# A two-layer decoder trunk: weights split in their own place, eight raw weight places among the experts, and the last expert's share by a product instead of a gather

## The chip, the cores and the metric

One core of a Trainium2 chip runs the whole kernel as one program. The metric is the time of one execution in microseconds of device time (lower is better). Five engines work side by side, each through its own instruction stream and held together by semaphores that the kernel sets by hand: PE (matrix products, with weight loads shown apart as PEld), DVE (vector), ACT (scalar), POOL (GpSimd) and SP, which here only issues DMA transfers.

## The reference

Two groups of tokens, 512 of a prompt and 32 of samples, run together as T = 544 columns of width D = 1024. Layer 0 mixes tokens with a gated linear recurrence (RG-LRU), layer 1 with a gated delta rule (GDN). Each layer then attends to 256 memory tokens and ends in a channel mixer: layer 0 a dense SwiGLU, layer 1 the best two of eight expert SwiGLUs.

```python
def _trunk(x, mem_k, mem_v, lru_h, lru_conv, gdn_s, gdn_conv, p):
    for i in range(DEPTH):                       # DEPTH = 2
        if i % 2 == 0: mix, h, c = _rglru_mixer(x, ...)
        else:          mix, s, c = _gdn_mixer(x, ...)
        x = _layer_norm(DN_ALPHA * x + mix, ...)
        xa = _mem_attention(x, mem_k[i], mem_v[i], p['xa_wq'][i], p['xa_wo'][i])
        x = _layer_norm(DN_ALPHA * x + xa, ...)
        if i % 2 == 0: ff = _swiglu(x, w_gu, w_down, D_FF)          # 3072 hidden
        else:          ff = _moe_ffn(x, router, w_gu, w_down)       # 8 experts of 1536, top 2
        x = _layer_norm(DN_ALPHA * x + ff, ...)
```

`_moe_ffn` takes the softmax of a token's two best router logits as its two weights and adds the two experts' outputs with them.

## The kernel before

Weights lie in DRAM as slots of 128 x 1024 fp32 (512 KB), each one output tile of 128 columns (or its counterpart of a down projection). All 488 slots pass through one ring `raw` of four places, filled by SP in the order in which PE will use them. Stages in that order: key/value tiles of the memory (KV0), four LRU blocks, the LRU output (LOUT), queries and output of the first attention (Q, O), the dense SwiGLU in two halves of 36 slots (FFN), 32 GDN slots (four for each head), the GDN output (GOUT), Q and O of the second attention, and 8 x 36 slots of the experts. Key/value tiles of layer 1 lie between stages and fill PE's time in layer norms.

**Dense slots** are used in two parts. POOL makes a high part `wh` (fp32r) in four instructions (L527) and a low part `wl`, the raw weights less the high part, in four more (L531). PE then runs 48 matmuls of 272 columns (`lin_steps`, L625; in the FFN's down projection L865): high weights times high activations, low weights times high activations, high weights times low activations. `wh` and `wl` have two places each, so POOL waits in `split` until PE is through with the slot two before (`w_used`). SP refills a raw place as soon as POOL has split it (`w_split`). Key/value slots are used raw and never split. After a layer norm the first two slots of Q and FFN run interleaved on PE, because the normalised tiles arrive one by one (`linear`, `experts`); the first two slots of GOUT run together in the same way (`opening`), begun before the last head's output is there.

**Experts.** Tokens are sorted by expert into `rows_x` in DRAM. Experts stand in the order of their size with capacities 208 to 128 rows. The four largest (`wide_expert`) split their weights: ACT makes the high part, DVE the low part, into four places of their own. The four smallest (`expert`) use the raw weights in plain fp32 (L1235 up, L1252 down). SP refills a raw place when DVE has made its low part or, in the small experts, when PE has used it. A small expert's up projection gives two slots for each of 12 hidden tiles: ACT takes the silu (L1820), DVE multiplies (L2445, signalling `m_h`), and PE waits for that two tiles later. In its down projection the output tiles are evicted by ACT, turned by PE (`turn`, L1218) and copied by DVE (`turned`, L2438) into `M_y`. POOL stores `M_y` to `rows_y` in DRAM (L591).

**The end.** After the last expert's store has landed, POOL issues ten indirect gathers (L604), two for each of five token blocks (four of 128, one of 32), of the rows of each token's two experts. DVE adds them with their weights to the residual in two passes of 1024 columns (`statistics`, L2554), takes mean and variance (L2556, L2557) and normalises (L2562); PE turns the block back (L1327); ACT applies gain and bias in eight instructions (`columns`, L1874) and issues the store of y (L1877). On ACT the order is: factor of block t+1, then columns of block t.

Of the kernel before, what the change touches and what calls it, by code (L numbers as in the profile page):

```python
# [37 lines left out]
RAW, SPLIT, PIECES = 4, 2, 4  # L38
# [3 lines left out]
ZEROS = -(-ROWS // P)  # L42
PICKED, GATHERED = 6, 2
# [78 lines left out]
def trunk(nc, I, O):  # L122
# [5 lines left out]
    with ExitStack() as ctx:  # L128
# [14 lines left out]
        wh = sb("wh", [P, SPLIT, KT, P], R)  # L143
        wl = sb("wl", [P, SPLIT, KT, P], R)
# [286 lines left out]
        def _(sp):  # L431
            def load(t, offset, shift, lo=0, hi=RAW):


                for j in range(lo, hi):
# [7 lines left out]
            def turns(slot, n, before, own, dram):  # L443
                t0 = slot // RAW
                load(t0, before, dram - slot)
                if n > RAW:
                    with sp.Fori(t0 + 1, t0 + n // RAW) as t:
                        load(t, own, dram - slot)
# [9 lines left out]
            load(0, None, W_KV0)  # L458
            sp.wait_ge(w_in[0], 16)
            sp.dma_start(x[:, :, :], I["xT"]).then_inc(ld_x, 16)  # L460
            turns(S_KV0[1], RAW, None, None, W_KV0 + 4)
            turns(S_LRU[0], 2 * RAW, None, 8, W_LRU)
            turns(S_KV0[2], RAW, 8, None, W_KV0 + 8)
            turns(S_LRU[2], RAW, None, None, W_LRU + 8)
            turns(S_LRU[3], RAW, 12, None, W_LRU + 12)
            turns(S_KV0[3], RAW, 12, None, W_KV0 + 12)
            turns(S_LOUT, 8, None, 16, W_LOUT)
            turns(S_KV1[0], 4, 16, None, W_KV1)
            for l in range(NL):
                d = (20, 32)[l]  # L470
                turns(S_Q[l], 8, None, d, W_Q0 if l == 0 else W_Q1)
                turns(S_O[l], RAW, d, d, (W_Q0 if l == 0 else W_Q1) + 8)
                cache(l)
                turns(S_O[l] + RAW, RAW, d, d, (W_Q0 if l == 0 else W_Q1) + 8 + RAW)
                if l == 0:
                    turns(S_KV1[1], 4, 20, None, W_KV1 + 4)
                    turns(S_FFN, HALVES * 36, None, 24, W_FFN)
                    turns(S_KV1[2], 4, 24, None, W_KV1 + 8)
                    turns(S_GDN, 4 * GH + 8, None, 28, W_GDN)
                    turns(S_KV1[3], 4, 28, None, W_KV1 + 12)  # L480
# [20 lines left out]
            with sp.Else():  # L501
                for n in range(RAW, NE * 36):
                    if n - RAW < WIDE * 36:
                        sp.wait_ge(m_wl, WL + n + 1 - RAW)
                    else:
                        sp.wait_ge(w_used, S_MOE + n + 1 - RAW)
                    expert_slot(n)
# [5 lines left out]
        def _(pool):  # L513
# [4 lines left out]
            def split(t, first, offset):  # L518
# [15 lines left out]
            def turns(slot, n, first, offset):  # L534
                t0 = slot // RAW
                split(t0, first, offset)
# [6 lines left out]
            turns(S_Q[0], 16, 4, 20)  # L543
            turns(S_FFN, HALVES * 36, 4, 24)
            turns(S_GDN, 4 * GH + 8, 4, 28)
            turns(S_Q[1], S_MOE - S_Q[1], 4, 32)
# [5 lines left out]
            with pool.Else():  # L552
# [47 lines left out]
                pool.wait_ge(m_out, OUT_BY[NE - 1])  # L600
                for tt in range(NT):
                    n = P if tt < NC else NS
                    for m in range(2):
                        nc.gpsimd.indirect_dma_start(  # L604
                            out=Y_in[tt][m][0:n, :], out_offset=None, in_=rows_y,
                            in_offset=bass.IndirectOffsetOnAxis(ap=R_slot[0:n, m, tt:tt + 1], axis=0)).then_inc(c_in_y[tt], 16)
# [4 lines left out]
        def _(pe):  # L611
# [50 lines left out]
            def linear(slot, direct, ah, al, freed, base, fresh=None, opened=False):  # L662
# [9 lines left out]
                for s in range(2 if opened or fresh is not None else 0, 8):  # L672
                    if s >= 2:
                        pe.wait_ge(freed, base + s - 1)
                    lin_tile(slot + s, direct, s % 2, s % 2, ah, al)
# [142 lines left out]
            def experts(n, slot, direct, e0, first_ln):  # L818

                def one(e):  # L820
                    e36, e12, e8 = e * 36 + slot, (e + e0) * FT, (e + e0) * KT

                    def up(g):
# [12 lines left out]
                        for j in range(2 if opening else 0, 4):  # L836
# [3 lines left out]
                            lin_tile(e36 + g * 4 + j, direct, j % 2, j, xh, xl)  # L840
# [11 lines left out]
                    def down(g):  # L852
                        for q in range(4 * FT):
# [9 lines left out]
                            for m, (w, a) in enumerate(w_parts):  # L863
                                for h in range(2):
                                    last = mm(ps[:, 2 * d + h, 0:HT], w[:, s % 2, k, :], a[:, f, h * HT:(h + 1) * HT],  # L865
# [4 lines left out]
                    if isinstance(e, int) and e + e0 == 0:  # L870
                        down(0)
                        down(1)
                    else:
                        with pe.Fori(0, 2) as g:
                            down(g)
# [3 lines left out]
            def project(h, per=6, fresh=None):  # L879

                for j in range(4):
# [4 lines left out]
                    yield from lin_steps(S_GDN + 4 * h + j, 28, j % 2, 0, xh, xl, per=per, fresh=None if j else fresh)  # L886
# [11 lines left out]
            def lru_gel(b):  # L898

                for j in range(2):  # L900
                    pe.wait_ge(lru_ext, 2 * b + j + 1)
                    lin_tile(S_LRU[b] + 2 + j, 8 + 4 * (b // 2), j, j, xh, xl)
# [319 lines left out]

            def expert(r):
# [3 lines left out]
                for q in range(24):  # L1227
# [5 lines left out]
                    pe.wait_ge(w_in[slot % RAW], 16 * (slot // RAW + 1))  # L1233
# [1458 lines left out]
```

## Time and profile before

| | us |
|---|---|
| median of 3 runs (2505.19 to 2506.25) | 2506.08 |
| the profiled execution | 2509.16 |
| its span between first and last instruction | 2507.3 |
| PE busy | 2291.6 (91% of the span) |
| POOL busy | 1063.6 (42%) |

The profiled execution took 1.86 us more than its span, and 3.08 us more than the median of the runs. Times of the trace count from the span's start. By them the dense SwiGLU runs from about 470 to 923 us, the GDN stage to about 1530 us, GOUT to 1578 us, the experts' products from 1834 to 2459 us, and what follows them to 2507 us. A matmul's busy time is modelled and matmuls overlap, so PE at 100% means only that there was no gap.

### The profile page before, as it was taken

To read this page: it belongs to the slowest core of one execution; us is meant where nothing else is said; L and a number is where in the kernel's file an instruction comes from. 1 tells how busy PE (TensorE), PEld (TensorE's weight loads), DVE (VectorE), ACT (ScalarE), POOL (GpSimd) and SP (SyncE) were. 2 spreads that over 40 slices of the span, in tenths; PEclk is the share of its full clock that TensorE was granted. 3 is DMA by queue.
4 is the path that set the end of the run, shared out by engine and by line. 5 is a ranking of instruction groups with operands and counts; after the bars stand their busy time and mean duration, and the time that the engine had idled before them with its cause. 6 is when DMAs were issued, how large, how long until landed. Compare 5 with 4: busy or idle time off the path is not lost.

```text
span 2507.3 us, 43919 instructions
## 1 busy us (share of the span) xinstructions
PE 2291.6 (91%) x17238; PEld 2165.0 (86%) x17238; DVE 1134.6 (45%) x1739; ACT 720.5 (29%) x1218; POOL 1063.6 (42%) x1483
## 2 busy tenths in 40 slices
PE   8998889899999998999999778888799999999993
PEld 8988867899999996888888667867699999999993
DVE  3684412411011147777777644412557777410004
ACT  2352321311001114333333311321355666411103
POOL 4657434588888875433333105534221232100001
PEclk9999899899999998999999988999699999999996
DMA  7214442222222222211121102541176777778884
GB/s 296 100 60 162 154 165 85 93 84 84 89 88 84 89 90 69 69 55 62 62 63 63 45 27 88 194 165 68 52 256 208 260 249 264 238 247 280 285 285 161
DMA packets 98515, 347.22 MB, mean 138 GB/s; under 512 B 13488, under 2 KB 18864, under 8 KB 93472
## 3 DMA queue, kind: packets, MB, share of 16 engines
q1 hardware_dynamic: 73136, 279.08, 31.9%
q10 hardware_dynamic: 19472, 45.28, 5.2%
q0 software_dynamic: 5728, 20.38, 2.2%
q8 instruction: 122, 2.00, 0.3%
q14 instruction: 57, 0.47, 0.1%
HBM read 318.25 MB, written 26.47 MB: 137 GB/s over the span
## 4 chain that ended last, share of the span: by engine, by line
PE 64%; issue 15%; DVE 9%; POOL 6%; ACT 3%; DMA 3%; ACTq 0%; DVEq 0%; POOLq 0%; SPq 0%
PE ps L625 26%; PE ps L1262 8%; PE ps L1235 6%; PE ps L865 4%; PE ps L1264 4%; POOL wl L531 3%; PE ps L1252 3%; POOL wh L527 2%; DMA raw<-weights 2%; PE ps L726 1%; DVE x L1953 1%; PE ps L1076 1%; PE ps L1072 1%; PE ps L1055 1%; PE ps L730 1%
## 5 line engine op out<-in xcount | busy, mean ns | idle before, releaser
L527 POOL TENSOR_TENSOR wh<-raw,tab 128x256 fp32r<-128x256 f32 x672 | 438.8, 684 | 807.4 <-PE ps L625 543.5
L531 POOL TENSOR_TENSOR wl<-raw,wh 128x256 fp32r<-128x256 f32 x672 | 522.1, 808 | 0.0
L625 PE MATMUL ps<-xh,wh 128*128 128x272 f32 x2048 | 306.5, 300 | 47.1 <-POOL wl L531 15.5
L625 PEld LDWEIGHTS ps<-xh,wh 128*128 128x128 f32 x2048 | 276.8, 195 | 61.9 <-issue 24.5
L625 PE MATMUL ps<-xh,wl 128*128 128x272 f32 x2048 | 298.7, 296 | 0.0
L625 PE MATMUL ps<-xl,wh 128*128 128x272 f32 x2048 | 281.0, 289 | 0.0
L625 PEld LDWEIGHTS ps<-xh,wl 128*128 128x128 f32 x2048 | 277.1, 195 | 1.8 <-issue 0.5
L625 PEld LDWEIGHTS ps<-xl,wh 128*128 128x128 f32 x2048 | 266.2, 189 | 0.0
L1262 PE MATMUL ps<-moe_x,moe_wh 128*128 128x416 f32 (+3 forms) x768 | 214.5, 356 | 4.8 <-DVE moe_wl L2458 3.5
L2458 DVE TENSOR_TENSOR moe_wl<-raw,moe_wh 128x1024 fp32r<-128x1024 f32 x144 | 178.1, 1237 | 52.1 <-ACT moe_wh L1832 49.1
L1264 PE MATMUL ps<-moe_x,moe_wl 128*128 128x208 f32 (+3 forms) x768 | 188.9, 246 | 0.0
L1832 ACT ACTIVATE moe_wh<-raw 128x1024 fp32r<-128x1024 f32 x144 | 152.8, 1061 | 40.6 <-DMA raw<-weights 28.3
L1262 PEld LDWEIGHTS ps<-moe_x,moe_wh 128*128 128x128 f32 x768 | 144.1, 188 | 6.2 <-issue 3.4
L1264 PEld LDWEIGHTS ps<-moe_x,moe_wl 128*128 128x128 f32 x768 | 146.6, 191 | 0.0
L577 POOL CAST moe_hs<-work 128x208 fp32r<-128x208 f32 (+3 forms) x44 | 49.2, 1118 | 214.9 <-DVE work L2484 214.9
L591 POOL DMA_DIRECT2D rows_y<-moe_h x8 | 4.4, 549 | 319.7 <-DVE moe_h L2438 319.7
L2037 DVE TENSOR_TENSOR work<-work,ps 128x544 f32<-128x544 f32 x24 | 17.3, 722 | 228.6 <-PE ps L625 228.6
L1262 PE MATMUL ps<-moe_hs,moe_wh 128*128 128x416 f32 (+3 forms) x384 | 110.5, 360 | 0.0
L1235 PE MATMUL ps<-x,raw 128*128 128x144 f32 (+1 forms) x768 | 93.4, 284 | 3.6 <-DMA raw<-weights 3.6
L1235 PEld LDWEIGHTS ps<-x,raw 128*128 128x128 f32 x768 | 92.3, 194 | 4.3 <-issue 3.1
L1264 PE MATMUL ps<-moe_hs,moe_wl 128*128 128x208 f32 (+3 forms) x384 | 94.7, 247 | 0.0
L1252 PE MATMUL ps<-work,raw 128*128 128x128 f32 (+2 forms) x768 | 93.7, 279 | 1.0 <-DVE work L2445 0.8
(407 smaller groups left out, 3901.4 us busy)
## 6 DMA issues: line engine op xcount, KB each, us to landing
raw<-weights SPq DMA_DIRECT2D x488, 512.0 KB, 4.2
moe_h<-cache SPq DMA_DIRECT2D x6, 2048.0 KB, 8.6
moe_h<-cache ACTq DMA_DIRECT2D x4, 2048.0 KB, 14.9
work<-cache SPq DMA_DIRECT2D x4, 2048.0 KB, 8.0
moe_h<-rows_x POOLq DMA_DIRECT2D x12, 512.0 KB, 8.1
rows_x<-lnsq ACTq DMA_DIRECT2D x9, 512.0 KB, 11.1
work<-scratch ACTq DMA_DIRECT2D x16, 272.0 KB, 4.2
work<-cache ACTq DMA_DIRECT2D x2, 2048.0 KB, 10.4
```

Of the source, the lines that this page charges most:

```text
L527: nc.gpsimd.tensor_tensor(flat(h1[:, k0:k1]), flat(r1[:, k0:k1]), one_col, MUL).then_inc(pool_hi, 1)
L531: low = nc.gpsimd.tensor_tensor(flat(l1[:, k0:k1]), flat(r1[:, k0:k1]), flat(h1[:, k0:k1]).bitcast(F), SUB)
L577: nc.gpsimd.tensor_copy(own[:, f, 0, :], M_hf[:, f % 2, 0:c]).then_inc(m_hp, 1)
L625: last = mm(ps[:, 2 * i + h, 0:HT], w[:, par_, k, :], a[:, k, h * HT:(h + 1) * HT], start=(n == 0 and k == 0), stop=(n == 2 and k == KT - 1))
L726: last = mm(ps[:, b, 0:MEM], raw[:, q, k, :], A_mem[:, k, :], start=(k == 0), stop=(k == KT - 1))
L865: last = mm(ps[:, 2 * d + h, 0:HT], w[:, s % 2, k, :], a[:, f, h * HT:(h + 1) * HT], start=(f == 0 and m == 0), stop=(f == FT - 1 and m == 2))
L1235: last = mm(ps[:, j // 2, (j % 2) * c:(j % 2 + 1) * c], raw[:, slot % RAW, k, :], own[:, k, :], start=(k == 0), stop=(k == KT - 1))
L1252: last = mm(ps[:, 2 + d % 2, 0:c], raw[:, slot % RAW, k, :], hid[:, f, :], start=(f == 0), stop=(f == FT - 1))
L1262: mm(ps[:, bank, 0:2 * c], moe_wh[:, rel % SPLITS, k, :], moving.rearrange("p a c -> p (a c)"), start=first, stop=False)
L1264: return mm(ps[:, bank, 0:c], moe_wl[:, rel % SPLITS, k, :], moving[:, 0, :], start=False, stop=last_one)
L1832: s(A(moe_wh[:, n % SPLITS], raw[:, slot % RAW], ACT.Copy), m_wh, WH + n + 1)
L2458: s(V.tensor_tensor(moe_wl[:, n % SPLITS], raw[:, slot % RAW], moe_wh[:, n % SPLITS].bitcast(F), SUB), m_wl, WL + n + 1)
```

## The change

Four things change; the same values are computed.

1. **Split in place.** `wl` becomes another name for `raw`: POOL writes the low part over the raw weights. `wh` grows to four places in the room that is saved. A raw place is now free only when PE has used the slot, so every load of SP waits for `w_used` of the slot four before.
2. **Splitting ahead.** For Q, O, FFN and GOUT (`ahead=True`) POOL no longer waits for PE at all, only for the load. LRU, LOUT and the GDN heads keep the pace of two (`PACE`).
3. **Eight raw places among the experts.** There the dense layers' four `wh` places are not used; as `raw2` they become four more raw places, so the ring holds eight slots.
4. **The end.** The last expert's rows are neither stored nor gathered. Its share of each token is a product: `shares` builds, before the first expert, a matrix that holds a token's weight at its row of the last expert; PE turns it (`turn_shares`), and after the last expert multiplies it with `M_y` (`last_products`). The gathers of the first seven experts' rows run during the last expert, and DVE adds them there (`combine`), one block after each of the last five hidden tiles. `statistics` then adds only the product. In the last two blocks DVE does half of ACT's columns.

PE's code of the FFN's down projection is also written out instead of looped, as the place now depends on the step.

The core of the diff:

```diff
-        wh = sb("wh", [P, SPLIT, KT, P], R)
-        wl = sb("wl", [P, SPLIT, KT, P], R)
+        wl = nc.alloc_sbuf_tensor_at("wl", [P, RAW, KT, P], R, offset=nc.sbuf_base - 4 * RAW * KT * P)
+        wh = sb("wh", [P, RAW, KT, P], R)
+        raw2 = nc.alloc_sbuf_tensor_at("raw2", [P, RAW, KT, P], F, offset=nc.sbuf_base - 4 * RAW * KT * P)
...
+        def place(n):
+            return (raw, raw2)[n % (2 * RAW) // RAW][:, n % RAW]
...
-                    if offset is None:
-                        ge(sp, w_used, t * RAW + (j + 1 - RAW))
-                    else:
-                        ge(sp, w_split, t * RAW + (j + 1 - RAW - offset))
+                    ge(sp, w_used, t * RAW + (j + 1 - RAW))
...
                 for n in range(RAW, NE * 36):
-                    if n - RAW < WIDE * 36:
-                        sp.wait_ge(m_wl, WL + n + 1 - RAW)
+                    before = n - 2 * RAW
+                    if before < 0:
+                        sp.wait_ge(w_used, S_MOE)
+                    elif before < WIDE * 36:
+                        sp.wait_ge(m_wl, WL + before + 1)
                     else:
-                        sp.wait_ge(w_used, S_MOE + n + 1 - RAW)
+                        sp.wait_ge(w_used, S_MOE + before + 1)
...
                     pool.wait_ge(w_in[j], t * 16 + 16)
-                    ge(pool, w_used, t * RAW + (j + 1 - SPLIT - (first if j < SPLIT else 0)))
-                    h1, l1, r1 = wh[:, j % SPLIT], wl[:, j % SPLIT], raw[:, j]
+                    if not ahead:
+                        ge(pool, w_used, t * RAW + (j + 1 - PACE - (direct if j < PACE else 0)))
+                    h1, l1, r1 = wh[:, j], wl[:, j], raw[:, j]
...
+                    if r == NE - 1:
+                        continue
                     pool.wait_ge(m_ye, KT * (r + 1))
                     pool.dma_start(rows_y[b:b + P, :], M_y[:, 0, :]).then_inc(m_out, 16)
...
-                pool.wait_ge(m_out, OUT_BY[NE - 1])
+                pool.wait_ge(m_x, NE - 1)
+                pool.wait_ge(m_out, OUT_BY[NE - 2])
...
+            def turn_shares():
+                pe.wait_ge(r_dve, SHARED + 1)
+                pe.wait_ge(m_xe, KT // 2 * NE)
+                for tt in range(NT):
+                    n = P if tt < NC else NS
+                    last = nc.tensor.transpose(ps[:, 6 + tt // NC, (tt % NC) * P:(tt % NC) * P + n], Z_share[0:n, tt, :], ident[0:n, 0:n])
+                last.then_inc(r_pe, 1)
+            def last_products(tt):
+                n = P if tt < NC else NS
+                for hf in range(2):
+                    if tt >= 2:
+                        pe.wait_ge(c_stat, tt - 1)
+                    last = mm(ps[0:n, 4 + 2 * (tt % 2) + hf, :], Z_turned[:, tt * P:tt * P + n], M_y[:, 0, 512 * hf:512 * hf + 512],
+                              start=True, stop=True)
+                last.then_inc(r_pe, 1)
...
+            def combine(tt):
+                n = P if tt < NC else NS
+                z = T_x[0:n, tt, :]
+                dve.wait_ge(c_in_y[tt], 32)
+                for m in range(2):
+                    s(V.scalar_tensor_tensor(z, Y_in[tt][m][0:n, :], Z_w[0:n, m, tt:tt + 1], z, MUL, ADD))
...
+                    if r == NE - 1 and f >= FT - NT:
+                        combine(f - (FT - NT))
...
+                    s(V.tensor_tensor(z, z, ps[0:n, 4 + 2 * (tt % 2):6 + 2 * (tt % 2), :], ADD))
...
+                def half_columns(tt):
+                    n = P if tt < NC else NS
+                    dve.wait_ge(c_tr, 2 * tt + 2)
+                    for i in range(4):
+                        k = 4 + i
+                        s(V.tensor_scalar(x[:, k, tt * P:tt * P + n], ps[:, 2 * (tt % 2) + 1, i * P:i * P + n],
+                                          pc("lng", 40 + k, 41 + k), pc("lnb", 40 + k, 41 + k), MUL, ADD),
+                          *((m_sum, SUM + WIDE * FT + tt - NC + 2) if i == 3 else ()))
```

`shares` is 26 small DVE instructions (11 on 5 or 10 columns, 15 on 128 columns) between `low_rows(0)` and the first expert's work.

## Rows read from the trace of the kernel before

**Rows 1.** The page's head: the span.

```profile
span 2507.3 us, 43919 instructions
```

**Rows 2.** Busy time by window: PE, PEld, DVE, ACT, POOL, granted clock, DMA share, GB/s.

```profile
450.00:500.00 50.00, 42.57 (x235) 39.08 (x234) 24.24 (x31) 20.25 (x27) 24.09 (x32) 0.86 0.25 93
550.00:600.00 50.00, 50.00 (x399) 50.00 (x398) 7.33 (x8) 5.51 (x9) 44.45 (x68) 1.00 0.25 91
2400.00:2450.00 50.00, 48.27 (x428) 47.79 (x428) 4.05 (x14) 3.88 (x14) 0.00 (x0) 1.00 0.84 289
2450.00:2500.00 50.00, 17.72 (x117) 15.61 (x116) 26.00 (x34) 19.00 (x46) 10.94 (x11) 0.61 0.46 157
```

**Rows 3.** PE's waits, whole span: us in total, times, longest us.

```profile
PE ps L625 <- POOL wl L531: 24.5, 21, 6.5
PE ps L1235 <- DMA raw<-weights: 6.9, 4, 2.7
PE ps L1262 <- DVE moe_wl L2458: 3.5, 3, 1.9
```

**Rows 4.** PE's waits between 100 and 260 us, the LRU stage.

```profile
PE ps L625 <- POOL wl L531: 3.0, 5, 1.8
```

**Rows 5.** Timeline: PE's stalls at Q, FFN, GOUT, second Q; POOL before GOUT.

```profile
297.46 3.96 PE L625 MATMUL ps<-xh,wh 128*128 128x272 f32 x16 [3.34 <-POOL wl L531]
301.23 3.26 PE L625 MATMUL ps<-xh,wl 128*128 128x272 f32 x16
304.32 2.17 PE L625 MATMUL ps<-xl,wh 128*128 128x272 f32 x16
...
492.50 4.00 PE L625 MATMUL ps<-xh,wh 128*128 128x272 f32 x16 [3.75 <-POOL wl L531]
...
1529.61 2.81 POOL L527 TENSOR_TENSOR wh<-raw,tab 128x256 fp32r<-128x256 f32 x4 [115.65 <-PE ps L654]
...
1536.73 3.96 PE L625 MATMUL ps<-hh,wh 128*128 128x272 f32 x16 [6.45 <-POOL wl L531]
...
1616.19 2.25 PE L625 MATMUL ps<-xh,wh 128*128 128x272 f32 x16 [3.34 <-POOL wl L531]
```

**Rows 6.** Timeline: POOL and DVE, alone and while both work.

```profile
277.53 1.07 DVE L1953 TENSOR_TENSOR x<-x,lnr 128x544 f32<-128x544 f32 x1
279.39 0.73 DVE L1953 TENSOR_TENSOR x<-x,lnr 128x544 f32<-128x544 f32 x1
...
294.55 2.77 POOL L531 TENSOR_TENSOR wl<-raw,wh 128x256 fp32r<-128x256 f32 x4
...
1568.53 3.30 POOL L531 TENSOR_TENSOR wl<-raw,wh 128x256 fp32r<-128x256 f32 x4
```

**Rows 7.** DMA landing: FFN loads; Q loads beside cache transfers; small experts' stores.

```profile
raw<-weights SPq DMA_DIRECT2D x65, 512.0 KB, 3.5
...
DMA to landing us min/median/max: 3.5/3.5/6.4
...
rows_y<-moe_h POOLq DMA_DIRECT2D x4, 512.0 KB, 5.1
```

**Rows 8.** Timeline: first expert's first eviction; last expert; the end.

```profile
1839.30 0.52 ACT L1842 ACTIVATE work<-ps 128x416 f32<-128x416 f32 x1 [5.90 <-PE ps L1264]
...
2432.08 0.29 DVE L2445 TENSOR_TENSOR work<-moe_h,ps 128x128 f32<-128x128 f32 x1 [3.28 <-ACT moe_h L1820]
...
2458.89 0.33 PE L1218 MATMUL ps<-tab,moe_h 128*128 128x128 f32 x1 [0.42 <-ACT moe_h L1812]
...
2463.07 1.04 POOL L604 DMA_INDIRECT moe_x<-rows_y,work  x1 [2.63 <-DMA rows_y<-moe_h]
...
2469.86 2.61 DVE L2554 SCALAR_TENSOR_TENSOR moe_h<-moe_x,work,moe_h 128x1024 f32<-128x1024 f32 x2 [10.24 <-DMA moe_x<-rows_y,work]
...
2480.62 3.90 ACT L1874 ACTIVATE x<-ps,par 128x128 f32<-128x128 f32 x8 [1.49 <-PE ps L1327]
...
2504.48 0.54 ACTq L1877 DMA_DIRECT2D out_y<-x  x1
```

More of the change, by code:

```diff
@@ L532, in split, with turns @@
                     low.then_inc(w_split, 1)
-            def turns(slot, n, first, offset):
+            def turns(slot, n, direct, offset, ahead=False):
                 t0 = slot // RAW
-                split(t0, first, offset)
+                split(t0, direct, offset, ahead)
                 if n > RAW:
@@ L542, in _ @@
             turns(S_LOUT, 8, 4, 16)
[L543 to L546, printed above, removed]
+            turns(S_Q[0], 16, 4, 20, ahead=True)
+            turns(S_FFN, HALVES * 36, 4, 24, ahead=True)
+            turns(S_GDN, 4 * GH, 4, 28)
+            turns(S_GDN + 4 * GH, 8, 0, 28, ahead=True)
+            turns(S_Q[1], S_MOE - S_Q[1], 4, 32, ahead=True)
             pool.wait_ge(r_dve, COUNTED)
@@ L869, in one @@
                     pe.sem_inc(passed, 1)
[L870 to L875, printed above, removed]
+                    down(0)
+                    down(1)
                 repeat(pe, n, one)
@@ L1232, in expert @@
                         pe.wait_ge(m_yt, KT * r - 3 + q // 2)
-                    pe.wait_ge(w_in[slot % RAW], 16 * (slot // RAW + 1))
+                    pe.wait_ge(*arrived(slot - S_MOE))
                     for k in range(KT):
-                        last = mm(ps[:, j // 2, (j % 2) * c:(j % 2 + 1) * c], raw[:, slot % RAW, k, :], own[:, k, :],
+                        last = mm(ps[:, j // 2, (j % 2) * c:(j % 2 + 1) * c], place(slot - S_MOE)[:, k, :], own[:, k, :],
                                   start=(k == 0), stop=(k == KT - 1))
@@ L1248, in expert @@
                     if k == 0:
-                        pe.wait_ge(w_in[slot % RAW], 16 * (slot // RAW + 1))
+                        pe.wait_ge(*arrived(slot - S_MOE))
                     if f == 0 and d >= 2:
                         pe.wait_ge(m_yt, r * KT + (d - 1))
-                    last = mm(ps[:, 2 + d % 2, 0:c], raw[:, slot % RAW, k, :], hid[:, f, :],
+                    last = mm(ps[:, 2 + d % 2, 0:c], place(slot - S_MOE)[:, k, :], hid[:, f, :],
                               start=(f == 0), stop=(f == FT - 1))
@@ L1829, in high_weights @@
                     slot = S_MOE + n
-                    act.wait_ge(w_in[slot % RAW], 16 * (slot // RAW + 1))
+                    act.wait_ge(*arrived(n))
                     act.wait_ge(w_used, S_MOE if n < SPLITS else slot + 1 - SPLITS)
-                    s(A(moe_wh[:, n % SPLITS], raw[:, slot % RAW], ACT.Copy), m_wh, WH + n + 1)
+                    s(A(moe_wh[:, n % SPLITS], place(n), ACT.Copy), m_wh, WH + n + 1)
             def wide_expert(r):
@@ L1869, in columns @@
                 n = P if tt < NC else NS
-                for hf in range(2):
+                for hf in range(2 if tt < NC - 1 else 1):
                     act.wait_ge(c_tr, 2 * tt + hf + 1)
@@ L2457, in low_weights @@
                     dve.wait_ge(m_wh, WH + n + 1)
-                    s(V.tensor_tensor(moe_wl[:, n % SPLITS], raw[:, slot % RAW], moe_wh[:, n % SPLITS].bitcast(F), SUB), m_wl, WL + n + 1)
+                    s(V.tensor_tensor(moe_wl[:, n % SPLITS], place(n), moe_wh[:, n % SPLITS].bitcast(F), SUB), m_wl, WL + n + 1)
             def low_rows(r):
@@ L2539, in _ @@
                 low_rows(0)
+                shares()
                 for r in range(NE):
```

116 lines of the change are left out of this document (78 added, 38 removed).

## The prediction

> **What bounds the kernel now.** I read the page's head first, then busy time by windows, PE's waits, the timeline at each of those waits, and at last the end. The span is 2507.3 us [rows 1]. In the dense SwiGLU PE has no gap and the granted clock is 1.00; POOL is busy for 44.45 of 50 us there [rows 2]. PE runs 399 matmuls in 50 us, so a slot of 48 takes 6.01 us of PE; POOL's 68 instructions make 5.23 us for the eight of a slot. POOL is faster than PE, so in steady state a deeper ring of split weights has nothing to give. In the small experts PE is busy for 48.27 of 50 us [rows 2]. What is to be had is therefore single stalls and the end, where PE is busy for 17.72 of 50 us.
>
> PE's waits give the stalls [rows 3]: 24.5 us for POOL's low parts in dense slots, 6.9 us for raw weights in the small experts, 3.5 us for DVE's low parts in the large ones (late behind the same loads). Of the 24.5, 16.9 us are four stalls, at the opening of Q, FFN, GOUT and the second Q: 3.34, 3.75, 6.45 and 3.34 us [rows 5]. The pattern is one: two slots finish on PE nearly together, and only the first of these finishings lets POOL begin the third slot, about 5.2 us of work, of which PE covers two. Before GOUT POOL had stood idle for 115.65 us for that one release.
>
> The reader should also see what follows a stall. After that at Q, 16 matmuls take 3.96 us and the next 16 take 3.26, against 2.17 once it is past [rows 5]: the clock had fallen to its lower level (1.2 instead of 2.4 GHz). FFN and GOUT begin in the same way, at 4.00 and 3.96 us; the window round FFN's opening shows a mean granted clock of 0.86 [rows 2, 5]. The second Q begins at 2.25 us after a stall of the same length: a stall does not always cost the clock.
>
> **The change, part by part.**
>
> *Splitting ahead, at the openings.* The third and fourth slot can be split while PE still waits for the normalised tiles. The stalls at Q, FFN and second Q go: 3.34 + 3.75 + 3.34 = 10.4 us. For the clock I add 3.96 + 3.26 - 2 x 2.17 = 2.9 us at Q and 2.7 at FFN (4.00 there, the second 16 taken as at Q). Nothing but the stall stopped PE there, so I take both; the bound is 0.
>
> At GOUT 6.45 us and 2.8 us of clock go, and up to 1.6 us of small waits in the rest of it. But there the stall moves on. Loads now wait for PE, so the fifth slot's load leaves when PE has used the first, just before POOL's start in the row at 1529.61. It lands 3.5 to 6.4 us later [rows 7]. POOL takes four times 0.83 us for either part while DVE works on the residual (3.30 against 2.77 us [rows 6]), 6.6 us a slot, more than PE's 6.0. PE reaches the fifth slot 12.0 us after it began the third. So that slot is ready 2 us early or 1 us late, and each later slot is 0.6 us later still: by the eighth the loss is 0 to 2.8 us. I take 1.1 off: 9.8 us, bounds 6.5 and 10.9. Sum of the openings: 10.4 + 5.6 + 9.8 = 25.8.
>
> *The rest of the waits on POOL.* 24.5 - 16.9 = 7.6 us, of which 3.0 lie in the LRU stage [rows 4], where the pace stays, and 1.6 are counted at GOUT. Of the remaining 3.0 I take 2.4; both bounds, 0 and 3.0, stay.
>
> *In place, later loads.* A raw place is held until PE has used it. In FFN a load leaves three slots, 18.0 us, before its need, lands after 3.5 us [rows 7] and is split in 5.2: over 9 us are left. After an opening the fifth slot has two slots' time, 12.0 us, plus the 2.0 us by which the second outlasts the first: beside cache transfers 6.4 + 5.2 = 11.6 us [rows 7] fit, by 2.4. Behind SP's waiting load stand the next loads and, in attention, the cache transfers; these wait for PE's later scores anyway. Cost 0. The extra POOL work meets DVE in the layer norms: two more slots beside the eight low parts of the activations. A DVE product with both inputs in SBUF took 1.07 us beside POOL and 0.73 without [rows 6]; eight times 0.34 is 2.7 us for each of three openings, if the path runs there. PE comes to the low parts last, so I take 0 and keep 8.2 for the range.
>
> The Trainium skill (SBUF — State Buffer, section Who interferes with whom) says that such a DVE instruction and a GpSimd instruction that reads SBUF exclude each other, the later one waiting until the other is through. That speaks against this change, and the 0.34 us agree with it in kind. By the rule a DVE instruction could wait out a whole POOL instruction, 0.69 us by the 2.77 for four; the three openings would then pay 16.6 us instead of 8.2, and the sum would be a gain of 35 us.
>
> *Eight raw places.* The small experts run at 289 GB/s with the DMA engines busy for 0.84 [rows 2], so single loads are late, not all of them: the longest wait is 2.7 us, and four more places hold some 7 us. 6.9 + 3.5 = 10.4 us; I take 10.0, lower bound 5.
>
> *The work brought forward.* `shares`, 26 DVE instructions at an estimated 0.25 us (0.29 for a product of 128 columns [rows 8]), is 6.5 us. DVE is free from the start of the first expert until its first eviction at 1839.30, which PE needs 5.90 us to reach [rows 8]; the rest delays it by about 1 us, and PE has two more slots to work on. Cost 0, bound 2. The turning of the shares is five transposes: 1.0 us of PE (0.33 for the one at 2458.89 as an upper price of each). `combine` takes 2.61 us after a hidden tile; DVE idles for 3.28 us between two [rows 8]. It fits while the gathers are there; behind it stands the next tile's product, for which PE waits two tiles later. The gathers start when the seventh expert's store has landed: two tiles of 3.57 us and 5.1 us [rows 7] after the last expert's start, 12.5 us. Ten issues at some 1.3 us end at 25.5. The first block's two took about 6 us in the quiet end (issue at 2463.07, first sum at 2469.86 [rows 8]); allow 11 among the weights. First block: 26 against 28.6 us; last: 36.5 against 43. Cost 0.
>
> *The end.* Before, from the last transpose at 2458.89 to the first sum at 2469.86 there are store, issue and gather. Now PE multiplies the first block right after the copy: two products of 512 columns. That transpose of 128 took 0.33 us, so each takes at most 1.3; as matmuls overlap I take 0.85. The first sum starts at about 2461.6. The two passes of 2.61 us become one of about 1.3, twice before the first columns. These begin at 2480.62 - (2469.86 - 2461.6) - 2 x 1.3 = 2469.8, 10.8 us earlier. ACT then sets the pace with 3.90 us a block. It loses four of eight instructions in the last two blocks, 1.95 + 1.6 us, and some 0.5 us of waiting for the small block's late statistics. The last store leaves 14.9 us earlier than 2504.48. The mean granted clock here is 0.61 [rows 2]; products at the lower level would take twice 1.7 us for a block and hold DVE up once or twice. I take 14.0, bounds 10 and 15.5.
>
> *Written-out code.* The down projection's first half was already written out and ran without a gap [rows 2]. Cost 0.
>
> **Sum.** 25.8 + 2.4 + 10.0 + 14.0 - 1.0 = 51.2 us. Against the profiled execution, 2509.16 (span 2507.3 and 1.86 around it), that is 2458.0. The median of the runs, 2506.08, lies 3.1 lower; so the prediction is 2454.9 us, 2.0% less.
>
> **Rivals.**
>
> *Half the openings' gain is lost* (17%): the stall moves to a late fifth slot or to slowed DVE work. For it: POOL's 6.6 us beside DVE and the 2.4 us of slack. Against it: loads land in 3.5 us, and low parts are wanted last. Price: 8.2 us for DVE and 5.6 for a clock that falls anyway, some 14: 2469.
>
> *The gathers starve the weights* (8%). Gathers are 4.5 MB; weights already take 289 of about 344 GB/s (289 / 0.84). If both halve that, 26 us of it leave the weights 3.0 MB, 5.8 slots, behind. Eight places just hold that; with a lead of four, PE waits some 4 us, and DVE's late sums add 3: 2462. The Trainium skill (DMA: Bandwidth & Descriptors, section Queues, rings and completion order) says that a DMA engine takes turns between the queues that have work, which is this rival's condition; no run here shows it yet.
>
> *Slower* (4%): POOL's subtraction onto its own input takes longer. No row shows one on POOL; DVE's L1953 works in place at 0.73 us [rows 6]. From 0.2 us more per instruction POOL takes over 6.0 us a slot and sets the pace of FFN, Q, O and GOUT, 112 slots. The gain is gone when a slot takes 51 / 112 = 0.46 us beyond that, 0.31 us more per instruction. At 0.4: 112 x 0.83 = 93 us, less 51: about 2548.
>
> *No change* (3%): the stalls go, but the waits come back at the next exchange with ACT or DVE, and the end waits for late gathers: 2506.
>
> **How the numbers follow.** My forecast has 68%: 2446 to 2464. Two runs can be told apart by about 0.2%, 5 us. The upper end takes in the first two rivals and a small end (10) with few gains in the experts (5): 2454.9 + 14 + 4 + 5 = 2478, little of which comes together, so 2475. The lower end takes every upper bound: 2446. Faster 0.93, within 0.2% 0.03, slower 0.04.
>
> **What would show it.** PE's waits on POOL outside the LRU stage should fall from over 20 us to below 4, the 16 matmuls after each opening should take 2.2 us, PE's waits on raw weights should be near 0, and between the last transpose and the last store there should be 31 us instead of 45.6. I am wrong if POOL's subtraction takes over 0.9 us with DVE idle, if PE waits for the fifth slot of a stage, or if in the last expert PE waits for DVE's products.

## The result and the profile after

The changed kernel takes 2475.8 us (median of four runs, 2469.0 to 2479.5) against 2505.6 us for the kernel before on the same chip: ratio 0.9879, 95% interval 0.9853 to 0.9904. The forecast was 2454.9 us, with a range to 2475: the direction was right, and some 21 us of the 51 did not come. The profiled execution took 2479.2 us.

The head of the page [rows 1]:

```profile
span 2477.3 us, 43914 instructions
```

PE's waits over the whole span: us in total, times, longest [rows 3]:

```profile
PE ps L647 <- POOL wl L549: 7.5, 17, 1.8
PE ps L1272 <- DMA raw<-weights: 2.9, 2, 1.7
PE ps L1301 <- DVE moe_wl L2535: 0.4, 1, 0.4
```

PE's timeline at the openings of Q, FFN and GOUT [rows 5]:

```profile
297.63 2.17 PE L647 MATMUL ps<-xh,wh 128*128 128x272 f32 x16
...
310.09 2.24 PE L647 MATMUL ps<-xh,wh 128*128 128x272 f32 x16 [0.22 <-POOL wl L549]
...
485.71 2.17 PE L647 MATMUL ps<-xh,wh 128*128 128x272 f32 x16
...
1533.84 2.26 PE L647 MATMUL ps<-hh,wh 128*128 128x272 f32 x16
```

What the change was to remove is gone: the third slot at Q begins without a wait and at the full clock (2.17 us for 16 matmuls, 3.96 before), and so do FFN's and GOUT's. Q's fifth slot (310.09) is 0.22 us late. Of the 7.5 us of waits for POOL, 4.5 lie before the first layer norm, where the pace stays. Waits for raw weights fell from 6.9 to 2.9 us.

One thing on the change itself has to be set right. `turns` hands `ahead` only to its first `split`, so POOL runs ahead in the first four slots of Q, FFN, GOUT and the second Q alone; the later slots of these stages, and all of O, keep the pace of two. The timeline of POOL shows it at Q's seventh slot and at GOUT's fifth, where it waits for PE and not for a load:

```profile
316.41 2.33 POOL L545 TENSOR_TENSOR wh<-raw,tab 128x256 fp32r<-128x256 f32 x4 [1.29 <-PE ps L647]
...
1540.25 3.29 POOL L545 TENSOR_TENSOR wh<-raw,tab 128x256 fp32r<-128x256 f32 x4 [116.57 <-PE ps L647]
```

The four openings that the forecast priced lie in those first four slots.

So the missing time must be where the forecast had put nothing. I set marks that both kernels have (a layer norm's first sum over partitions, each head's update of the samples' states, the first expert's rows, the last transpose, the last store) and took the length of each stretch, in us, as a difference to the first profile of before. "Again" is a second profile of the changed kernel, "held" the version of the third experiment.

| stretch | forecast | after | again | held |
|---|---|---|---|---|
| start to first layer norm | 0 | +3.6 | +0.9 | +3.0 |
| Q, attention, O | -6.2 | -6.4 | -7.3 | -5.5 |
| FFN | -6.4 | -6.9 | -7.5 | -7.6 |
| delta rule to the fifth head | 0 | +6.5 | +1.6 | -0.3 |
| sixth head | 0 | +6.6 | +4.2 | 0.0 |
| last two heads | 0 | 0.0 | -1.8 | +0.8 |
| GOUT | -9.8 | -8.8 | -8.7 | -7.7 |
| second Q, attention, O | -3.3 | -2.0 | -2.2 | -4.0 |
| routing | 0 | -1.5 | -1.4 | -1.4 |
| first expert's rows | 0 | +4.2 | +4.3 | +4.1 |
| experts | -9.0 | -10.4 | -8.9 | -10.7 |
| last transpose to last store | -14.0 | -14.8 | -14.8 | -14.8 |
| sum (forecast: with 2.4 of small waits) | -51.2 | -30.0 | -41.5 | -44.1 |

In both profiles of the changed kernel, every stretch that the forecast priced came within 2 us of it. The loss stands in rows with a forecast of 0: in the delta-rule stage 13.1 us in one profile and 4.0 in the other, and in the first expert's rows over 4 in both. The sixth head is the last one of the delta rule with a projection beside it. Busy time by windows of that head, before (behind the columns of PE, PEld, DVE, ACT and POOL stands the granted clock):

```profile
1340.50:1403.80 63.30, 59.69 (x483) 55.34 (x482) 46.27 (x81) 21.54 (x43) 21.92 (x32) 1.00 0.19 62
```

And after:

```profile
1337.00:1407.00 70.00, 63.76 (x476) 59.45 (x475) 49.20 (x81) 21.16 (x42) 35.50 (x48) 0.92 0.20 57
```

DVE has the same 81 instructions, POOL 48 instead of 32: two more of GOUT's splits moved in here. The timeline of POOL, DVE and PE there, in the changed kernel:

```profile
1374.29 4.19 POOL L549 TENSOR_TENSOR wl<-raw,wh 128x256 fp32r<-128x256 f32 x4
...
1373.89 0.99 DVE L2247 TENSOR_TENSOR work<-work 128x512 f32<-128x512 f32 x1
1374.91 0.59 DVE L2248 TENSOR_TENSOR work<-work 32x32 f32<-32x32 f32 x1
1375.54 1.19 DVE L2290 TENSOR_TENSOR work<-work,lnr 128x544 f32<-128x544 f32 x1
...
1377.93 0.69 DVE L2361 TENSOR_TENSOR work<-ps,moe_h 128x512 f32<-128x512 f32 x1
...
1378.67 1.91 PE L1090 MATMUL ps<-work 128*128 128x128 f32 x8 [2.16 <-DVE work L2361]
```

POOL's four subtractions take 4.19 us instead of 2.8, and the DVE products beside them lengthen as well, so DVE comes to L2361 late; PE waits 2.16 us for it and then runs the 8 matmuls in 1.91 us. Without the splits it waits 0.65 us and runs them in 1.16, as the same place shows in the held version (the third experiment; here its repetition, in which this line is L1092):

```profile
1371.33 1.16 PE L1092 MATMUL ps<-work 128*128 128x128 f32 x8 [0.65 <-DVE work L2363]
```

The granted clock of the changed kernel was 1.00 to 1377 us, 0.89 from there to 1392, and 0.75 to 1407.

### The profile page after: what moved, and what is told of

It is laid out like the page before. It is cut to its first block, busy times and chain, and to the rows that moved or that the text cites. A ratio compares the mean times of both kernels' runs of the same rounds, so it can differ in the third digit from the quotient of the medians.

```text
span 2477.3 us, 43914 instructions
## 1 busy us (share of the span) xinstructions
PE 2296.8 (93%) x17263; PEld 2166.8 (87%) x17263; DVE 1160.4 (47%) x1780; ACT 717.2 (29%) x1210; POOL 1078.8 (44%) x1482
## 4 chain that ended last, share of the span: by engine, by line
PE 69%; DVE 11%; issue 9%; POOL 5%; ACT 3%; DMA 1%; ACTq 1%; DVEq 0%; POOLq 0%; SPq 0%
PE ps L647 26%; PE ps L1301 9%; PE ps L1272 7%; PE ps L887 4%; PE ps L1303 4%; PE ps L1291 4%; POOL wl L549 3%; POOL wh L545 2%; PE ps L1094 2%; PE ps L1090 2%; PE ps L748 2%; PE ps L1073 1%; DVE x L2000 1%; PE ps L1220 1%; DMA raw<-weights 1%
## 5 line engine op out<-in xcount | busy, mean ns | idle before, releaser
L545 POOL TENSOR_TENSOR wh<-raw,tab 128x256 fp32r<-128x256 f32 x672 | 448.7, 698 | 787.5 <-PE ps L647 594.8
L1877 ACT ACTIVATE moe_wh<-raw 128x1024 fp32r<-128x1024 f32 x144 | 152.8, 1061 | 25.3 <-DMA raw<-weights 12.4
L1291 PEld LDWEIGHTS ps<-work,raw 128*128 128x128 f32 x768 | 90.9, 191 | 1.4 <-DVE work L2516 1.4
L1272 PE MATMUL ps<-work,raw 128*128 128x136 f32 (+1 forms) x768 | 88.7, 277 | 2.9 <-DMA raw<-weights 2.9
```

Source lines behind the costliest of these rows:

```text
L545: nc.gpsimd.tensor_tensor(flat(h1[:, k0:k1]), flat(r1[:, k0:k1]), one_col, MUL).then_inc(pool_hi, 1)
L1272: last = mm(ps[:, j // 2, (j % 2) * c:(j % 2 + 1) * c], place(slot - S_MOE)[:, k, :], own[:, k, :], start=(k == 0), stop=(k == KT - 1))
L1291: last = mm(ps[:, 2 + d % 2, 0:c], place(slot - S_MOE)[:, k, :], hid[:, f, :], start=(f == 0), stop=(f == FT - 1))
L1877: s(A(moe_wh[:, n % SPLITS], place(n), ACT.Copy), m_wh, WH + n + 1)
```

## The experiments

**The changed kernel again.**

> The changed kernel once more, nothing edited. Three theories stand for the 13.8 us that the delta-rule stage lost. Early splits: GOUT's weights, split while the last head with a projection beside it still runs, slow VectorE there and TensorE's clock falls; the stretch of 69.9 us against 63.3 (6.6 us) must then come back in this second profile at much the same size. Ring: the loads that wait for TensorE are late throughout the stage; then all heads are longer by some 1 to 2 us, in this profile as in the first. Chance: the clock falls now and then whatever the kernel does; then the lost time sits elsewhere or is gone in this profile, and the times scatter by 10 us as the first ones did. The 3.6 us at the start and the 2.7 us in the routing are chance if they do not come back.

2473.9 us (2467.6 to 2474.8), ratio 0.9861 (0.9836 to 0.9885). The sixth head is 4.2 us longer than before; the head before it is back at 63.3 us. So the sixth head's loss is of the kernel. The first heads' 6.5 us shrank to 1.6, and they are not of GOUT's splits: the profile of a later version in which those are held (both together, below) shows them again, in the same heads (3.8, 1.4 and 1.4 us), with its sixth head at 63.3 us. In both profiles the 3.8 us go with longer waits of PE for ACT ahead of the first head's mark (9.7 and some 4 us, against 7.8 and 2.4 before), the other two with a clock of 0.97 in two heads. What lengthens those waits is open.

**GOUT at the old pace.**

```
-            turns(S_GDN, 4 * GH, 4, 28)
-            turns(S_GDN + 4 * GH, 8, 0, 28, ahead=True)
+            turns(S_GDN, 4 * GH + 8, 4, 28)
```

> The changed kernel, but GOUT's weights are split at the pace of before (two slots ahead of TensorE), all else as changed. Early splits: the head's stretch goes back to about 63.3 us (6.6 us back) and GOUT's opening loses the 9.5 us it gained, so about 3 us slower than the changed kernel. Ring or chance: nothing comes back in the stage and the opening is lost, so about 9.5 us slower.

2474.2 us, the same as the changed kernel on that chip (2473.9). The opening's gain is lost (GOUT as long as before, +0.1), and the delta rule is back at the length of before (heads within 0.2 us). Splitting ahead at GOUT gave nothing: it cost as much as it brought.

**GOUT's splits held.** The first two slots at the old pace, the other two after the last head's large products:

```
-                    if not ahead:
+                    if held is not None:
+                        pool.wait_ge(*held[j])
+                    elif not ahead:
...
-            turns(S_GDN + 4 * GH, 8, 0, 28, ahead=True)
+            turns(S_GDN + 4 * GH, 8, 0, 28, held=((w_used, S_GOUT - 1), (w_used, S_GOUT), (d_wt, GH), (d_wt, GH)))
```

> The changed kernel, but of GOUT's first four slots the first two are split at the pace of before and the other two only once the last head has made its last large products (about 15 us before the opening). Early splits: the stretch of 69.9 us goes to 63.3 or so and the opening keeps its 9.5 us, so about 6 us faster than the changed kernel, some 2469 us. Ring or chance: no difference, within 3 us of it.

2465.1 us, ratio 0.9823 (0.9800 to 0.9846): 8.8 us less than the changed kernel on the same chip. The sixth head is at 63.3 us again, and GOUT keeps 7.7 us of its gain. Busy time of the sixth head's window, from the repetition of this version below:

```profile
1329.20:1392.70 63.50, 59.89 (x484) 55.44 (x482) 46.49 (x83) 21.09 (x41) 21.86 (x32) 1.00 0.22 62
```

And the timeline of the same DVE instructions as above, now without POOL beside them (their line numbers are two higher), and of POOL's next split:

```profile
1368.06 0.69 DVE L2249 TENSOR_TENSOR work<-work 128x512 f32<-128x512 f32 x1
1368.78 0.18 DVE L2250 TENSOR_TENSOR work<-work 32x32 f32<-32x32 f32 x1
1369.00 0.73 DVE L2292 TENSOR_TENSOR work<-work,lnr 128x544 f32<-128x544 f32 x1
...
1491.68 2.32 POOL L547 TENSOR_TENSOR wh<-raw,tab 128x256 fp32r<-128x256 f32 x4 [86.75 <-PE ps L1107]
```

The 0.99, 0.59 and 1.19 us are 0.69, 0.18 and 0.73, the clock is 1.00, and POOL comes back at 1491.68 only. The ring's rule for the loads is the same in both versions, and GOUT's first two loads leave 18.6 and 31.8 us into the sixth head (18.5 and 31.8 in the changed kernel); so the loss came from POOL's work and not from the ring.

**All four held.**

```
-            turns(S_GDN + 4 * GH, 8, 0, 28, ahead=True)
+            turns(S_GDN + 4 * GH, 8, 0, 28, held=((d_wt, GH - 1), (d_wt, GH - 1), (d_wt, GH), (d_wt, GH)))
```

> As the one before, but the first two slots wait too, until the last head but one has made its large products; so no split of GOUT runs beside the last projection. Early splits: as good as the one before or a little better (the head may fall below 63.3 us, since before too had two splits there), 2466 to 2470 us. Ring or chance: within 3 us of the changed kernel.

2465.6 us: no further gain. The stretch of the seventh head gets 2.4 us shorter and the eighth's 3.2 us longer. That is not of the place of the splits: the version with 13 products below, which splits where the held one does, shows 2.4 and 2.9 us in the same two heads.

**Two of four ahead.**

```
-            turns(S_GDN + 4 * GH, 8, 0, 28, ahead=True)
+            turns(S_GDN + 4 * GH, 8, 0, 28, held=((w_used, S_GOUT - 3), (w_used, S_GOUT - 2), (d_wt, GH), (d_wt, GH)))
```

> As the version with GOUT's splits held, but the first two slots are split as soon as their loads have landed, as in the changed kernel; the other two stay held. Early splits: two of the four splits fall back into the last head with a projection beside it, which gets 2 to 5 us longer than 63.3, and the time lies between the two, 2 to 5 us above 2465. Rival: only the third and fourth split did the harm; then the same as held, within 1.5 us.

2468.1 us (2463.3 to 2474.7), 3.0 above the held version; its sixth head, with one split more (40 instructions of POOL against 32), is 2.0 us longer. Runs of one version lie up to 15 us apart, and the two intervals overlap (0.9818 to 0.9855 against 0.9800 to 0.9846), so the 3.0 us are not clear of noise; what speaks for early splits is the sixth head.

**The first stage unpaced too.**

```
-            turns(S_LRU[0], 2 * RAW, 8, 8)
+            turns(S_LRU[0], 2 * RAW, 8, 8, ahead=True)
```

(and so for the other LRU slots and LOUT, in every turn of the loop)

> The version with GOUT's splits held, and the recurrence stage's and its output's splits no longer paced: GpSimd splits a slot as soon as its load has landed. By the theory that the unpaced splits cost where VectorE's work lies on the path, this meets the convolutions and scans: TensorE's waits for GpSimd fall from 4.6 us to about 1, but VectorE's products get slower by up to half while GpSimd runs, so between 3 us faster and 6 us slower. Rival (only the stall of a full ring matters, VectorE has room): 3.5 us or more faster.

2472.4 us, 7.3 us slower, beyond my upper bound. All waits of PE for POOL in this stage are gone (4.6 us), and the first layer norm comes 5.6 us later. The timeline of DVE, POOL and PE shows the instruction behind it:

```profile
115.27 16.52 DVE L2138 TENSOR_SCALAR work<-work,par 128x568 f32<-128x568 f32 x1 [16.72 <-ACT work L1549]
...
126.36 2.34 POOL L547 TENSOR_TENSOR wh<-raw,tab 128x256 fp32r<-128x256 f32 x4
128.64 2.84 POOL L551 TENSOR_TENSOR wl<-raw,wh 128x256 fp32r<-128x256 f32 x4
...
152.16 3.99 PE L649 MATMUL ps<-xh,wh 128*128 128x272 f32 x16 [12.11 <-ACT work L1557]
```

A DVE instruction that takes 0.58 us a little later (at 135.27) needs 16.52 us here. It ends at 131.79, just after POOL's unbroken run of splits ends at 131.48. PE then waits 12.11 us for ACT, which is behind DVE.

**The kernel before again.**

> The kernel before, unedited, with a second profile. Two things of the first comparison are open: the changed kernel reached the first layer norm 0.9 to 5.1 us later in its profiles, and built the first expert's rows in 25.3 us (21.1 in the profile of before; 21.0 in one of the changed ones). If that is chance of the clock, this profile reaches the first layer norm some 1 to 4 us later than the first one, or builds the rows in over 22 us, with no edit at all. If it belongs to the change, both stand as in the first profile: 262.0 and 21.1 us.

2508.7 us. It reaches the first layer norm 3.1 us later than in its first profile, with no edit, and after the first attention it is level again, since Q's opening cost less clock (3.55 and 2.16 us for the two times 16 matmuls behind the stall, against 3.96 and 3.26 [rows 5]). So a delay of 3 us at the start comes without any edit; with two profiles of before (262.0 and 265.1 us) and 262.9 to 267.0 in the changed versions, a small share of the change is not excluded. The rows look less like chance: 21.1 us again, where ten of eleven profiles of changed versions show 23.5 to 25.5, and one 21.0.

**Four raw places among the experts** (on the held version):

```
-            return (raw, raw2)[n % (2 * RAW) // RAW][:, n % RAW]
+            return raw[:, n % RAW]
...
-                    before = n - 2 * RAW
+                    before = n - RAW
```

> The version with GOUT's splits held, but with four raw places among the experts, as before the change, instead of eight. By the forecast the eight places are worth 10.0 us, so this one is slower by 10 (5 to 13): about 2475 us against 2465, and TensorE waits for raw weights in the small experts for 7 us or more again. Rival: the gain there came from the rest (the earlier end of the stages before); then within 3 us, and the waits stay near 2 us.

2489.0 us, 23.9 slower than with eight. PE's waits, with four places:

```profile
PE ps L1272 <- DMA raw<-weights: 12.2, 10, 3.7
PE ps L1301 <- DVE moe_wl L2535: 3.1, 5, 1.1
```

Its profiled execution (2484.4 us) shows 18 us of that: from the turning of the second expert's rows to that of the eighth's 472.4 us against 461.6, and from there to the last transpose 101.1 against 94.1. The rest lies between runs. The eight places are worth more than the 10.0 us that I gave them.

**Half of the gathers** (on the held version):

```
-                    for m in range(2):
+                    for m in range(1):
...
-                    s(V.scalar_tensor_tensor(z, Y_in[tt][m][0:n, :], Z_w[0:n, m, tt:tt + 1], z, MUL, ADD))
+                    s(V.scalar_tensor_tensor(z, Y_in[tt][0][0:n, :], Z_w[0:n, m, tt:tt + 1], z, MUL, ADD))
```

> The version with GOUT's splits held, but each token gathers one expert row instead of two (the sum adds that one twice, so the output is not the reference's; VectorE's work is the same). Theory: the early gathers and the weights starve each other in the last expert, and that costs the 3 us of TensorE's waits for raw weights and up to 3 us of VectorE's wait for a gathered block; then both waits go and the time falls by 3 to 6 us. Rival: the gathers lie under the products as forecast and cost nothing; then no change, within 2 us.

2461.5 us, 3.6 us less. Between the medians that is not clear of noise (0.9799 to 0.9830 against 0.9800 to 0.9846); the profile says more: the last expert takes 90.9 us instead of 94.1, and neither PE nor DVE waits for a transfer in it. In the changed kernel those waits are these, in the timeline of DVE and PE:

```profile
2417.11 2.60 DVE L2484 SCALAR_TENSOR_TENSOR moe_h<-moe_x,work,moe_h 128x1024 f32<-128x1024 f32 x2 [3.39 <-DMA moe_x<-rows_y,work]
2414.26 2.02 PE L1272 MATMUL ps<-work,raw 128*128 128x128 f32 x16 [1.28 <-DMA raw<-weights]
2417.93 2.05 PE L1272 MATMUL ps<-work,raw 128*128 128x128 f32 x16 [1.65 <-DMA raw<-weights]
```

Loads of weights issued in that expert landed up to 15.4 us after their issue, against 6.2 in the last expert of before. The DMA view of a window in it, from 2360 to 2400 us, with the median us from issue to landing at the end:

```profile
moe_x<-rows_y,work POOLq DMA_INDIRECT x8, 13.0
```

**Both together.** The two edits above at once.

> Four raw places among the experts and half of the gathers together (GOUT's splits held; the output is not the reference's, since each token's second row is the first again). With all gathers, four places cost 24 us more than eight, where the forecast says 10. Starvation: the eight places are worth 10 us by themselves and some 14 because they cover the loads while the gathers run; with half of the gathers four places then cost 10 to 16 us over eight (2461.5), so 2472 to 2478. Rival: the places cost the same whatever the gathers do; then 24 us over it again, about 2485.

2487.1 us: the rival holds. Four places cost the same with half of the gathers (25.6 us over 2461.5; 474.4 us and 97.3 for the two stretches), so what eight places are worth above 10 us is not the cover they give the gathers. What it is stays open.

**A warm clock for the rows.** 13 products that nobody reads, ahead of the routing branch:

> The version with GOUT's splits held, and TensorE runs 13 extra products of 256 columns, whose result nobody reads, before it builds the first expert's rows, in a gap of 6.6 us in which it waits for VectorE. The first rows take 25 us in most profiles of the changed versions and 21 in both of before, by when the clock rises. Clock: with the gap filled the clock rises sooner, the rows take 17 to 22 us, and the time falls by 3 to 8 us. Rival (the rows are slow for their data or for the loads beside them): they stay at 25 us, and the time is the same or some 1 us more.

2470.5 us, no gain. The timeline of PE:

```profile
1781.46 7.21 PE L1200 MATMUL ps<-x,tab 128*128 128x256 f32 x26
1792.87 22.89 PE L1225 MATMUL ps<-work,moe_h 128*128 128x208 f32 x80 [4.21 <-issue]
```

(Each product is counted twice.) The rows took 22.9 us, but began 4.6 us later after the last layer norm than in the held version: the branch's 4.21 us, hidden before under the wait for DVE, now stood behind the products. Inconclusive, so once more with 6 products behind the branch, beside the held version unedited:

```
             def first_rows():
                 pe.wait_ge(t_h, 2 * NT)
+                for _ in range(6):
+                    mm(ps[:, 0, 0:256], ident, x[:, 0, 0:256], start=True, stop=True)
```

> The version with GOUT's splits held, with 6 extra products of 256 columns (their result is not read) in the 3.3 us between TensorE's branch on the routing and the first product of the first expert's rows, so that nothing is delayed. The first try put 13 of them ahead of the branch, which then ended 3 us late. Clock: the clock rises some 3 us sooner after the first product; the rows take 21 to 23.5 us instead of 25.2, and the time falls by 1.5 to 4 us. Rival (the moment of the rise does not hang on these 3 us): rows at 25 us, the same time within 1.5 us.

> The version with GOUT's splits held, unedited, once more on the same chip, so that the other run has its own comparison: 2465 us again, within 4, and the last head with a projection beside it at 63.3 us again. If the head is longer this time, the 6 us that holding the splits gave back was chance.

2461.8 us (ratio 0.9826, 0.9813 to 0.9840) against 2465.4 for the held version, whose sixth head is at 63.3 us again. The rows take 18.5 us instead of 25.2, 6.7 us less in the profile; between the medians stand 3.6, with intervals that overlap (0.9819 to 0.9861 for the held version). The timeline of PE, products and rows:

```profile
1785.33 4.33 PE L1217 MATMUL ps<-x,tab 128*128 128x256 f32 x12 [3.07 <-issue]
1789.49 0.88 PE L1224 MATMUL ps<-work,moe_h 128*128 128x208 f32 x4
...
1799.79 8.21 PE L1224 MATMUL ps<-work,moe_h 128*128 128x208 f32 x38
```

What differs is the granted clock. Windows of the rows alone, in before, in the changed kernel, in the version with all four held and in this one (the last three columns are the granted clock, the share of the DMA engines and GB/s):

```profile
1811.70:1832.80 21.10, 21.08 (x80) 15.17 (x80) 9.89 (x15) 5.78 (x7) 6.07 (x7) 0.82 0.94 370
1802.70:1828.00 25.30, 25.27 (x80) 18.15 (x80) 9.91 (x15) 5.78 (x7) 8.49 (x11) 0.67 1.02 406
1793.40:1814.40 21.00, 20.98 (x80) 15.15 (x80) 9.75 (x15) 5.78 (x7) 6.42 (x7) 0.82 1.03 403
1789.50:1808.00 18.50, 17.76 (x81) 12.88 (x79) 9.25 (x14) 5.78 (x7) 7.07 (x6) 1.00 1.01 400
```

The times go with the clock and not with the loads, which are the same in the last three.

## Why the prediction was wrong

**The openings: right, and then paid for.** Q, FFN, GOUT and second Q gave 24 to 26 us with their attention stages, against 25.8. Part of that is luck of the profile: the 2.9 us of clock at Q were read from the first profile of before, and against the second, where Q's opening lost less clock, the Q stretch gained 3.1 and 4.0 us instead of 6.4 and 7.3, and the four openings 21 to 22. Two fifth slots were late, which the forecast named as a sign of being wrong: at Q by 0.22 us, where it had 2.4 of slack, and at GOUT by 0.85, where it had 2 early to 1 late (by the profile PE waited there for DVE; POOL's split ended 0.14 us before PE began). The DVE products in the layer norms cost nothing visible, as taken.

**In place, later loads: the step that failed.** I wrote "The extra POOL work meets DVE in the layer norms", and priced that meeting alone. But GOUT's four slots are free to be split as soon as the ring brings them, 120 to 150 us ahead of their use, and that is mostly the sixth head: three of the four ran there, against one before. DVE's chain there is what PE waits for, and a late PE lost its clock (0.92 over the head, 1.00 before). The row that I had (0.73 to 1.07 us [rows 6]) held there too, at 0.69 to 0.99 and 0.73 to 1.19; I asked where the wait would vanish, not where the work would land. The measured cost, where I had put 0, is 4.2 and 6.6 us in the two profiles and 8.8 between the medians. That holding the splits brings this back, and that the old pace brings it back at the price of the opening, shows the cause; that early splits of two slots cost 2.0 us of it in the sixth head agrees. It is not all of the 21 us: with the splits held some 9 us are still missing between the medians, and some 7 with the products ahead of the first expert's rows as well.

The Trainium skill (SBUF — State Buffer, section Who interferes with whom) has the rule for it: by it a DVE instruction with two SBUF inputs and a GpSimd instruction that reads SBUF exclude each other, and one with a PSUM input is spared. The trace agrees: beside the same splits L2361, which reads PSUM, stays at 0.69 us. The 16.6 us that the rule would have cost at the openings did not come.

**Rival 1**, half of the openings' gain lost to slowed DVE work, came near in size (2469), but not by its mechanism: the DVE work that was slowed stood a stage earlier. The rival by which POOL's subtraction onto its own input is slower did not come: it took 812 ns in the mean, 808 before.

**The sums.** FFN's 2.7 us of clock are right by the row of before (4.00 and 3.04 us for the two times 16 matmuls), but not "as at Q", where the second took 3.26. The range does not follow from its terms: the upper bounds add up to some 5 us of gain, which gives 2450 and not 2446, and the upper end names two rivals but adds only the first one's 14 us; the 7 of the second would have made it 2485. And 5 us do not tell two single runs apart here: those of one version lie up to 15 us apart.

**Experts: right sum, two sizes wrong.** Six of the experts got 13.6 us shorter than before (461.6 us against 475.1). By the two profiles with four places, 11 to 13 of these are the eight places', and 6 to 7 more in the last expert; I gave them 10.0 in all. The gathers, priced at 0, took 3.2 back in the last (rival 2, weighed at 8%: its wait of PE came at 2.9 us instead of 4, and DVE's at 3.4 instead of 3). That the two errors nearly cancel is luck. The failed line is "allow 11 among the weights": gathers landed after 13.0 us in the median; from a block's first issue to its second landing it was 11.6 us for the first block, but 21.1 for the fourth, at which DVE waited.

**The end: right.** 30.8 us from last transpose to last store, in every version, against 31 forecast. The timeline of the changed kernel's end [rows 8]:

```profile
2443.68 0.33 PE L1236 MATMUL ps<-tab,moe_h 128*128 128x128 f32 x1 [0.42 <-ACT moe_h L1857]
...
2474.46 0.54 ACTq L1924 DMA_DIRECT2D out_y<-x  x1
```

**The first expert's rows: not in the forecast.** The same 40 products, 4 us more, at a granted clock of 0.67 instead of 0.82. Filling PE's idle time ahead of them gave it back, at a clock of 1.00, so it is the clock; why it rises later in most profiles of the changed versions is open.

## What to carry to other kernels

When a change lets an engine run ahead, look up what runs beside the work at its new time, and price that by the rows in which the two engines already met; that the old wait goes says nothing on it. Give early work a release in a stretch where its neighbour has time, by an event of the program, not "as soon as possible". And a clock that falls after a stall makes single profiles differ by several us: profile both kernels twice before a term of 3 us is explained.

## What the hardware showed that I had not expected

- One engine can keep another out for much longer than one instruction: the DVE TENSOR_SCALAR of 0.58 us took 16.52 us beside some 24 POOL instructions and ended when their run did, while POOL ran on at its own pace (2.33 and 2.8 us for four). At other places in the same run both slowed together (0.94 us beside 4.05). What decides between the two is open. The Trainium skill (SBUF — State Buffer, section Who interferes with whom) has it that a TENSOR_SCALAR in a two-port mode and GpSimd block each other fully, for the whole instruction of the one that came first; no view shows which mode this one ran in, and that a block lasts over a whole run of instructions is this trace's.
- The same 40 products took 18.5, 21.0 or 25.3 us at a mean granted clock of 1.00, 0.82 or 0.67.
- A branch of PE on a loaded value shows as 3.07 and 4.21 us of "issue" (time in which the engine waited for nothing that the profile shows) in the two versions with extra products. In the held version it lay under PE's wait for DVE (6.86 us).
